# The final norm of a two-layer decoder step, done on rows in PSUM instead of on columns in SBUF

## The reference, cut to what matters

```python
def rmsnorm(x, g):
    xf = x.astype(jnp.float32)
    y = xf * lax.rsqrt(jnp.mean(xf * xf, axis=-1, keepdims=True) + EPS)
    return (y * g.astype(jnp.float32)).astype(x.dtype)
...
    for l in range(DEPTH):
        h = rmsnorm(x, norm_mix[l])
...
        x = x + y
        x = x + cross_attend(rmsnorm(x, norm_x[l]), mem_k[l], mem_v[l], w_q[l], w_o[l])
    return rmsnorm(x, final_norm), ...
```

## Time and profile before

| what | value |
|---|---|
| median of 3 runs | 2837.38 us (2836.62 to 2838.63) |
| the profiled execution's own time | 2837.96 us |
| its span (first to last instruction) | 2836.2 us |
| TensorE busy | 2584.4 us (91%) |
| VectorE busy | 1326.0 us (47%) |
| GpSimd busy | 990.0 us (35%) |
| ScalarE busy | 423.7 us (15%) |
| mean granted TensorE clock | 0.955 |

### The profile page before, as it was taken

One profiled execution on the slowest core, in us unless ns is written; L12 is line 12 of the kernel. 1 busy time (PEld: TensorE's weight loads), 2 busy tenths in 40 slices (PEclk: granted clock), 3 DMA queues, 4 the chain that ended last, 5 costly groups with the idle time before them and its releaser, 6 DMA issues. The chain is left out here.

```text
span 2836.2 us, 37082 instructions
## 1 busy us (share of the span) xinstructions
PE 2584.4 (91%) x14870; PEld 2438.1 (86%) x14870; DVE 1326.0 (47%) x1574; ACT 423.7 (15%) x720; POOL 990.0 (35%) x842
## 2 busy tenths in 40 slices
PE   4988989887996899999899999999999996999996
PEld 4988989787996787897799999999999996688786
DVE  5899999998443523223422222222222326232324
ACT  3111101111112211102200000000000013210112
POOL 2543434343334522333333333333333336133232
PEclk7999999999997899999899999999999998999998
DMA  2111111111121313321111111111111103132231
GB/s 91 54 45 47 55 45 52 47 48 57 61 73 38 106 37 100 115 73 53 49 42 46 45 42 44 45 45 41 45 45 44 42 26 103 51 112 61 86 107 63
DMA packets 224021, 168.61 MB, mean 59 GB/s; under 512 B 10746, under 2 KB 219138, under 8 KB 223922
## 3 DMA queue, kind: packets, MB, share of 16 engines
q1 hardware_dynamic: 214002, 156.78, 18.1%
q10 hardware_dynamic: 9920, 10.48, 1.1%
HBM read 152.29 MB, written 14.93 MB: 59 GB/s over the span
## 5 line engine op out<-in xcount | busy, mean ns | idle before, releaser
L144 POOL TENSOR_SCALAR w_hi<-w_raw 128x512 fp32r<-128x512 f32 x404 | 317.7, 786 | 1693.0 <-PE PS L205 1449.5
L205 PE MATMUL PS<-h_hi,w_hi 128*128 128x364 f32 x2880 | 645.6, 333 | 33.6 <-DVE e_V L822 11.6
L205 PE MATMUL PS<-h_hi,w_lo 128*128 128x364 f32 x2880 | 642.5, 332 | 0.0
L205 PE MATMUL PS<-h_lo,w_hi 128*128 128x364 f32 x2880 | 640.7, 331 | 0.0
L147 POOL TENSOR_TENSOR w_lo<-w_raw,w_hi 128x512 fp32r<-128x512 f32 x404 | 602.2, 1490 | 33.7
L205 PEld LDWEIGHTS PS<-h_hi,w_hi 128*128 128x128 f32 x2880 | 503.0, 190 | 38.3 <-issue 14.4
L205 PEld LDWEIGHTS PS<-h_hi,w_lo 128*128 128x128 f32 x2880 | 505.9, 190 | 0.0
L205 PEld LDWEIGHTS PS<-h_lo,w_hi 128*128 128x128 f32 x2880 | 504.6, 190 | 0.0
L845 DVE SCALAR_TENSOR_TENSOR e_C<-e_V,prm,e_C 128x1024 f32<-128x1024 f32 x240 | 314.4, 1310 | 0.3
L205 PE MATMUL PS<-y_hi,w_hi 128*128 128x364 f32 x1152 | 261.3, 335 | 53.9 <-ACT e_GS L696 24.3
L205 PE MATMUL PS<-y_hi,w_lo 128*128 128x364 f32 x1152 | 258.6, 333 | 0.0
(11 more groups left out here) (192 smaller groups left out, 2219.9 us busy)
## 6 DMA issues: line engine op xcount, KB each, us to landing
w_raw<-in_w_in_odd SPq DMA_DIRECT2D x128, 256.0 KB, 2.8
w_raw<-in_w_in_even SPq DMA_DIRECT2D x80, 256.0 KB, 3.0
a_KV<-in_cache_mem_k SPq DMA_DIRECT2D x64, 256.0 KB, 4.7
a_KV<-in_cache_mem_v SPq DMA_DIRECT2D x64, 256.0 KB, 3.3
w_raw<-in_w_out_even SPq DMA_DIRECT2D x32, 256.0 KB, 3.0
w_raw<-in_w_k SPq DMA_DIRECT2D x32, 256.0 KB, 2.8
w_raw<-in_w_v SPq DMA_DIRECT2D x32, 256.0 KB, 2.8
w_raw<-in_w_q SPq DMA_DIRECT2D x32, 256.0 KB, 2.7
```

What stands on the lines that cost most here:

```text
L144: c.nc.gpsimd.tensor_scalar(c.Wh[:, s, :], c.Wraw[:, s % RAW, :], 1.0, 1.0, ALU.mult, ALU.mult).then_inc(self.w_hi, 1)
L205: mm = pe.matmul(ps[:, q, 0:PART], w, a[:, q * PART:(q + 1) * PART], start=first and n == 0, stop=last and n == 2)
```

## The change

The final norm no longer uses the class Norm. The last cross block (layer 1) makes no squares and no sums any more. In the final block TensorE turns the unscaled residual into PSUM first, a tile of 128 rows (64 in the ninth) into one of four pairs of banks, with eight transposes. For each tile ScalarE squares the 1024 columns out of PSUM into a scratch buffer and lets the instruction sum each row; a second, small instruction takes the Sqrt of the mean plus eps. VectorE takes the reciprocal and then makes the output rows with one instruction: PSUM times the row's reciprocal times the gain, into y_rows. The gain must lie along the free dimension now, so SP loads the row of final_norm into all 128 partitions (y_gain) at the start of the block, ahead of the stores on its queue; VectorE waits for this load before its first instruction. TensorE reuses a pair of banks when the tile four back has been scaled. SP stores a tile when its one instruction is done.

```diff
 def block_final(c):
...
+        SQ = lay(c, "y_squares", [P, 2, D])
+        GB = lay(c, "y_gain", [P, D])
+        ST = lay(c, "y_rstd", [P, T // P + 1])
...
+        def pair(t):
+            return c.PS[0:rows(t), 2 * (t % 4):2 * (t % 4) + 2, :]
+
+        @block.tensor
+        def _(pe):
+            for t in range(tiles):
+                n = rows(t)
+                if t >= 4:
+                    pe.wait_ge(scaled, t - 3)
+                for k in range(KD):
+                    mm = pe.transpose(pair(t)[:, k // 4, P * (k % 4):P * (k % 4 + 1)],
+                                      c.X[:, k, t * P:t * P + n], c.ident[:, :])
+                mm.then_inc(turned, 1)
 
         @block.scalar
         def _(act):
-            norm.scalar_std(act)
             for t in range(tiles):
...
-                nc.scalar.activation(YN[0:n, t, 0:512], c.PS[0:n, 2 * (t % 2), :], ACT.Copy).then_inc(copied[0], 1)
...
+                act.wait_ge(turned, t + 1)
+                if t >= 2:
+                    act.wait_ge(squared, t - 1)
+                nc.scalar.activation(SQ[0:n, t % 2, :].rearrange("p (a n) -> p a n", a=2), pair(t), ACT.Square,
+                                     accum_out=ST[0:n, t:t + 1]).then_inc(squared, 1)
+                act.wait_ge(squared, t + 1)
+                nc.scalar.activation(ST[0:n, t:t + 1], ST[0:n, t:t + 1], ACT.Sqrt, bias=c.eps[0:n, 0:1],
+                                     scale=1.0 / D).then_inc(std, 1)
 
         @block.vector
         def _(dve):
-            norm.vector_rstd(dve)
...
-                    nc.vector.scalar_tensor_tensor(c.X[:, k, lo:hi], c.X[:, k, lo:hi], c.prm[:, k, ROW_FINAL:ROW_FINAL + 1],
-                                                   norm.R[:, lo:hi], ALU.mult, ALU.mult).then_inc(scaled, 1)
...
+            dve.wait_ge(gain_in, 16)
+            for t in range(tiles):
+                n = rows(t)
+                dve.wait_ge(std, t + 1)
+                nc.vector.reciprocal(ST[0:n, t:t + 1], ST[0:n, t:t + 1]).then_inc(inv, 1)
+                dve.wait_ge(inv, t + 1)
+                nc.vector.scalar_tensor_tensor(YN[0:n, t, :].rearrange("p (a n) -> p a n", a=2), pair(t), ST[0:n, t:t + 1],
+                                               GB[0:n, :].rearrange("p (a n) -> p a n", a=2),
+                                               ALU.mult, ALU.mult).then_inc(scaled, 1)
 
         @block.sync
         def _(sp):
+            sp.dma_start(GB[:, :], r["final_norm"].rearrange("(a d) -> a d", a=1).to_broadcast([P, D])).then_inc(gain_in, 16)
             for t in range(tiles):
-                sp.wait_ge(copied[0], t + 1)
-                sp.wait_ge(copied[1], t + 1)
+                sp.wait_ge(scaled, t + 1)
...
@@ block_cross
             G.split_all(pool, UNITS * NH)
-            norm.next_sums(pool)
+            if layer == 0:
+                norm.next_sums(pool)
...
             heads(act, head)
-            norm.next_squares(act, lambda k: wait_read(act, NH - 1, k))
+            if layer == 0:
+                norm.next_squares(act, lambda k: wait_read(act, NH - 1, k))
```

More of the change, by code:

```diff
@@ L436, in block_final, with rows @@
 def block_final(c):
-    nc = c.nc
+    nc, r = c.nc, c.dram
     c.at = c.region
     tiles = T // P + 1
-    THIRD = 3 * P
     with ExitStack() as ctx:
         sem = semaphores(c, ctx)
-        norm = Norm(c, sem)
         YN = lay(c, "y_rows", [P, T // P + 1, D])
-        scaled, turned, stored = sem("scaled"), sem("y_turned"), sem("y_stored")
-        copied = [sem("y_copied0"), sem("y_copied1")]
-        block = ctx.enter_context(nc.Block())
+        SQ = lay(c, "y_squares", [P, 2, D])
+        GB = lay(c, "y_gain", [P, D])
+        ST = lay(c, "y_rstd", [P, T // P + 1])
+        gain_in, turned, squared, std, inv = sem("gain_in"), sem("y_turned"), sem("y_squared"), sem("y_std"), sem("y_inv")
+        scaled, stored = sem("y_scaled"), sem("y_stored")
+        block = ctx.enter_context(nc.Block())
+        def rows(t):
+            return P if t < T // P else NS
+        def pair(t):
[10 more added lines that the diff above has]
+                mm.then_inc(turned, 1)
@@ L449, in _ @@
         @block.scalar
         def _(act):
-            norm.scalar_std(act)
             for t in range(tiles):
-                n = P if t < T // P else NS
-                act.wait_ge(turned, 2 * t + 1)
-                nc.scalar.activation(YN[0:n, t, 0:512], c.PS[0:n, 2 * (t % 2), :], ACT.Copy).then_inc(copied[0], 1)
[L457 to L471, removed]
+                n = rows(t)
@@ L473, in _ @@
         @block.vector
         def _(dve):
-            norm.vector_rstd(dve)
[L477 to L484, removed]
-                    nc.vector.scalar_tensor_tensor(c.X[:, k, lo:hi], c.X[:, k, lo:hi], c.prm[:, k, ROW_FINAL:ROW_FINAL + 1],
-                                                   norm.R[:, lo:hi], ALU.mult, ALU.mult).then_inc(scaled, 1)
-                if third:
-                    for t in range(3 * third - 3, 3 * third):
-                        copy(t)
@@ L490, in _ @@
-            for t in range(6, tiles):
-                copy(t)
+            dve.wait_ge(gain_in, 16)
+            for t in range(tiles):
+                n = rows(t)
+                dve.wait_ge(std, t + 1)
[4 more added lines that the diff above has]
+                                               ALU.mult, ALU.mult).then_inc(scaled, 1)
@@ L493, in _ @@
         @block.sync
         def _(sp):
+            sp.dma_start(GB[:, :], r["final_norm"].rearrange("(a d) -> a d", a=1).to_broadcast([P, D])).then_inc(gain_in, 16)
             for t in range(tiles):
-                sp.wait_ge(copied[0], t + 1)
-                sp.wait_ge(copied[1], t + 1)
+                sp.wait_ge(scaled, t + 1)
                 if t < T // P:
-                    sp.dma_start(c.dram["y_prompt"][0, t * P:(t + 1) * P, :], YN[:, t, :]).then_inc(stored, 16)
+                    sp.dma_start(r["y_prompt"][0, t * P:(t + 1) * P, :], YN[:, t, :]).then_inc(stored, 16)
@@ L500, in _ @@
                 else:
-                    sp.dma_start(c.dram["y_sample"].rearrange("b t d -> (b t) d"), YN[0:NS, t, :]).then_inc(stored, 16)
+                    sp.dma_start(r["y_sample"].rearrange("b t d -> (b t) d"), YN[0:NS, t, :]).then_inc(stored, 16)
             sp.wait_ge(stored, 16 * tiles)
```

## The result

The changed kernel takes **2820.47 us** (median of 4 runs, 2818.52 to 2822.98), the kernel before 2837.2 beside it: a ratio of 0.9941, 95% interval 0.9924 to 0.9958. Forecast were 2821.1, between 2817.5 and 2826.0, faster. The profiled execution of the changed kernel takes 2820.75 with a span of 2819.0.

A forecast was written before the change was run, and what follows sets the result against it. A serial tail of 39.59 us behind the last add bounds the kernel's end. Saving 3.84 at the turn and shortening the last block from 30.4 to 18.0 saves 16.25: 2837.38 - 16.25 = 2821.1 us, range 2817.5 to 2826.

The forecast's parts named there:

- The turn: Between last add and last block: without GpSimd's sums the block starts 1.0 us after the add, 3.84 us saved.
- The first tile: Start of the last block: transposes, Square, table load and Sqrt give the first standard deviation 3.88 us after the start.
- The gain row: Start of the last block: the 512 KB gain load lands after 4.5 us and releases VectorE, 0.6 behind the standard deviation.
- VectorE's pace: Last block: reciprocal 0.15, scaling 1.28 and gaps 0.06 make 1.50 us a tile, nine tiles 13.5.
- The stores: Last block: 1.29 us a tile hides under 1.50; the last store's 4.35 stays or shrinks by up to 0.5.
- The clock: TensorE's transposes in the last block: a half clock costs nothing, 0.5 us at most.
- the gain row was not late: Rival at the last block's start: repeated row reads delay the gain to 12.9 us, time 2829.5; 7 in 100.
- the table was loaded once: Rival on ScalarE: table reloads between Square and Sqrt, two 1.28 us loads a tile, time 2840.7, slower; 3 in 100.
- the stores did not set the pace: Rival in the last block: stores at two thirds rate, 1.94 us a tile, set the pace, time 2825; 6 in 100.
- the turn was GpSimd's: Rival at the turn: something other than GpSimd holds the block's end, start stays at 2801.44, time 2825; 3 in 100.

The follow-up runs named there:

- the turn put back: Changed kernel with the last cross block again making its unused squares and sums: 2825.34 us, ratio 0.9953 to the kernel before.
- both experiments on the turn: Changed kernel with unused squares and sums restored: 2825.34 us; old final block with only two of eight chunks squared and summed: 2833.02 us.
- the table load hidden: Changed kernel with a small Sqrt ahead of ScalarE's first wait in the last block: 2818.85 us, ratio 0.9931 to the kernel before.
- the merged kernel: Changed kernel with the final norm appended to the last cross block, first transposes following the adds, table and gain row loaded early: 2817.51 us, ratio 0.9927.
- five gain loads: Changed kernel with the gain row loaded five times into five buffers, VectorE waiting for all: 2827.27 us, ratio 0.9962 to the kernel before.
- most stores left out: Changed kernel without six of its eight prompt stores: 2820.63 us, ratio 0.9938 to the kernel before.

## Why the prediction was right

From the last add to the end the prediction's terms are 1.0 + 4.5 + 13.5 + 4.35 = 23.35. Measured are 1.13 + 3.93 + 12.58 + 4.26 = 21.90.

The mechanism came as described: the turn went with GpSimd's sum, the start-up is the pieces named, and VectorE's nine scalings set the pace. Two sizes, a releaser and a reading were off.

- **The turn** (1.0, bounds 0.8 and 1.13): 1.13, the upper bound. The first transpose comes about as long behind VectorE's add as behind GpSimd's sum (1.17 before the change and with the turn put back), so the row of the first block was the worse neighbour. That GpSimd held it is shown by both experiments on the turn.
- **The first tile**: transposes and first standard deviation at 3.88 behind the start; 2801.76 + 0.30 - 2798.2 = 3.86. The Square, its accumulator read and the one table load behind it came as in the earlier trace rows.
- **The gain row** (4.5, the start of VectorE): the one step that had the wrong releaser. It landed before the Sqrt, in less than 3.9; with the table load hidden its landing shows as 3.73. The 4.5 was the median of eight landings of 3.6 to 5.7, so 3.73 is no stranger among them; what sets the difference no run shows. Worth 0.6.
- **VectorE's pace** (1.50, bounds 1.45 to 1.57): 1.39, below the lower bound. The scaling is the 1.28 taken, but the reciprocal costs 0.08 + 0.02 on the chain instead of 0.15 + 0.06, because it starts while the scaling before it is still ending (the second one at 2803.56, while the first scaling, from 2802.36, ends at 2803.64). The first tile still takes 1.48; eight times 0.11 is 0.9. ScalarE overlaps likewise: its second Square starts at 2801.96, before the Sqrt ends at 2802.06, and its pace is 1.33 (2803.29 - 2801.96), not 1.45.
- **The stores** (hidden, last one 4.35): hidden, 4.26.
- **The clock** (nothing, 0.5 at most): nothing, but the price behind it was misread. The 4.12 for 20 transposes is not all at the half clock: the granted clock was 0.50 up to 2819.0 and 1.00 again from 2819.5. Eight at the half clock took 1.95 in the kernel with the turn put back, 0.87 more than at the full one. Nine times 1.95 would be 17.6, an estimate, more than VectorE's 12.6. The term came out at nothing because the block began at 1.00 and TensorE was four tiles ahead when VectorE started; with the turn put back it did cost 0.87.

The two sizes that were off, the start on VectorE (0.57) and its pace (0.92), make the tail 1.45 shorter than forecast, net of the turn and the last store. That the median lies only 0.6 below the forecast is luck: the profiled execution reached the last add 0.49 later, and the rest is where each profiled execution lies against its median. The pace lies below its bound, so the forecast's bounds held only because other terms had room (23.35 - 1.75 = 21.6 at the least, measured 21.9). The chances named, 81 for the forecast and 7, 3, 6 and 3 for the rivals, add up to 100 and leave nothing for what was not thought of. The rivals fell one by one: the gain row was not late, though perhaps by 0.15 only; the table was loaded once; the stores did not set the pace; the turn was GpSimd's.

## What to carry to other kernels

Look at what engine ends a block last: a helper that prepares the next block can hold the barrier, here for 3.7 us, and the idle time can also cost TensorE's clock in the next block. Where a serial tail is left, moving work to where each row's data already is, with one large instruction a tile on ScalarE and on VectorE, turns a chain of waits into a pipeline whose length is start-up plus pace. Then price the start-up piece by piece: here table load, turn and first transposes still held 3 us that the merged kernel took out.

## What the runs showed of the hardware that was not expected

- Small instructions behind a large one on the same engine overlap its end: a reciprocal of 0.15 adds 0.10 between two scalings, gap included, although the second scaling must wait for it.
- TensorE's clock in the last block differs between executions that look alike: with 2.47 us of idle time before the first transpose in both, the windows of the changed kernel show 1.00 from 2798.0 on, while those of five gain loads show 0.50 from 2800.0 to 2802.0, and 32 transposes took 3.69 and 5.35. With four pairs of banks a fall at that point cost the end nothing: with most stores left out the clock fell too, and the last scaling ended 17.65 behind the last add, in the changed kernel 17.64.
- Five loads in a row that each read one row 128 times moved at some 300 GB/s (313 and 299 in the two windows), plain rows at 391 and 369. A single such load reached 418 for half a us.
